# Issue order in a decoder trunk's attention and delta-rule stage: transposes and scores of a head pair next to each other

## The reference, cut to what matters

```python
s = jnp.einsum('bqhd,bkhd->bhqk', qn, k_nope) + jnp.einsum('bqhr,bkr->bhqk', qp, k_pe)
p = jax.nn.softmax(where(k_pos <= q_pos, s * scale, -inf), axis=-1)
o_a = jnp.einsum('bhqk,bkhd->bqhd', p, v)
...
sol = lax.linalg.triangular_solve(system, rhs, left_side=True, lower=True)   # per chunk
v_new = u_c - w_c @ state
o_c = q_c @ state + a_c @ v_new
state = state * exp(gl_c) + kd_c.T @ v_new
```

## Time and profile before

| | us |
|---|---|
| median of 3 runs | 2609.85 |
| lowest, highest | 2607.31, 2614.17 |
| the profiled execution's own time | 2610.53 |
| its span, first to last instruction | 2608.8 |
| PE busy in the span | 2342.1 (90%) |
| DVE, ACT, POOL busy | 1043.6 (40%), 913.8 (35%), 396.4 (15%) |
| mean granted TensorE clock | 0.949 |

### The profile page before, as it was taken

How to read it: one execution, slowest core, us unless ns; L and a number is a source line. 1 busy time by engine, 2 the same in 40 slices (tenths; PEclk the granted TensorE clock), 3 DMA queues, 4 the chain that set the end, 5 groups by cost and what they waited for, 6 DMA issues and landing times. The chain is left out here.

```text
span 2608.8 us, 47837 instructions
## 1 busy us (share of the span) xinstructions
PE 2342.1 (90%) x17450; PEld 1350.2 (52%) x17451; DVE 1043.6 (40%) x2320; ACT 913.8 (35%) x2284; POOL 396.4 (15%) x641
## 2 busy tenths in 40 slices
PE   6999999999588999999998998799974999999990
PEld 2545545555256666666666666355542444444440
DVE  2433433433345656666565556122225222222223
ACT  2273462634545545655554545111110101101103
POOL 1000000000100001000000000122320222222224
PEclk9999999999789999999999989899986999999995
DMA  9122121111443113221212103723321779999777
GB/s 336 71 65 68 47 84 47 59 50 49 128 121 96 59 52 93 82 66 53 69 64 83 36 30 147 266 105 121 116 77 33 211 203 285 283 323 300 230 238 285
DMA packets 187949, 334.34 MB, mean 128 GB/s; under 512 B 19788, under 2 KB 119783, under 8 KB 184567
## 3 DMA queue, kind: packets, MB, share of 16 engines
q1 hardware_dynamic: 173942, 281.51, 31.5%
q0 software_dynamic: 13824, 50.34, 8.0%
HBM read 242.36 MB, written 89.44 MB: 127 GB/s over the span
## 5 line engine op out<-in xcount | busy, mean ns | idle before, releaser
L688 PE MATMUL pV<-mod_rows_then_work,w_in_sb 128*128 128x512 f32 x768 | 340.4, 596 | 5.0 <-ACT mod_rows_then_work L357 5.0
L1416 PE MATMUL scores<-keys_values_then_all,queries 96*128 96x512 f32 (+3 forms) x640 | 311.0, 569 | 23.3 <-DMA keys_values_then_all<-v_d 23.3
L2030 PE MATMUL hidden_ps<-w,keys_values_then_all 128*128 x752 | 331.0, 593 | 0.1
L1136 ACT ACTIVATE probs<-scores,neg_max 128x512 f32<-128x512 f32 (+3 forms) x320 | 199.7, 624 | 341.9 <-DVE neg_max L1264 224.4
L688 PEld LDWEIGHTS pV<-mod_rows_then_work,w_in_sb 128*128 128x128 f32 x768 | 144.6, 191 | 178.0 <-issue 172.0
L2030 PEld LDWEIGHTS hidden_ps<-w,keys_values_then_all 128*128 128x128 f32 x752 | 143.0, 190 | 180.2 <-issue 180.2
L1617 PE MATMUL out_ps<-keys_values_then_all 128*128 128x512 f32 x512 | 227.8, 604 | 2.6 <-ACT keys_values_then_all L1560 2.6
L1421 PE MATMUL bank<-ident,probs 128*128 128x128 f32 x1088 | 188.0, 289 | 1.3 <-ACT probs L1136 1.1
L1264 DVE TENSOR_REDUCE neg_max<-scores 128x1 f32<-128x512 f32 x192 | 132.3, 689 | 133.0 <-PE scores L1416 131.7
L1431 PE MATMUL outT_ps<-probs_T,keys_values_then_all 128*64 128x128 f32 x2176 | 159.7, 286 | 28.5 <-issue 17.3
L1960 ACT ACTIVATE keys_values_then_all<-hidden_ps 128x256 f32<-128x256 f32 x47 | 18.1, 385 | 453.9 <-PE hidden_ps L2030 453.9
(11 more groups left out here) (361 smaller groups left out, 3283.1 us busy)
## 6 DMA issues: line engine op xcount, KB each, us to landing
w<-in_w_dram SPq DMA_DIRECT2D x64, 1024.0 KB
w_sb<-in_w_dram SPq DMA_DIRECT2D x32, 1024.0 KB
w_mod_rows<-in_w_mod_dram SPq DMA_DIRECT2D x16, 1024.0 KB, 4.9
kqv<-qkv_d SPq DMA_DIRECT2D x16, 768.0 KB, 4.4
mod_rows_then_work<-in_w_mod_dram SPq DMA_DIRECT2D x4, 2048.0 KB, 15.0
x_in<-in_x_dram SPq DMA_DIRECT2D x16, 512.0 KB, 4.9
qkv_d<-l_out SPq DMA_DIRECT2D x32, 256.0 KB, 2.3
keys_values_then_all<-y_d SPq DMA_DIRECT2D x16, 512.0 KB, 4.7
```

The source lines that it names most:

```text
L688: last = pe.matmul(pV[n % 2][:], win[:, k, QKV0 + c * P:QKV0 + (c + 1) * P], hT[:, s % 2, k, :], start=(k == 0), stop=(k == ND - 1))
L1136: act.activation(prob[:, e, 0:w].rearrange("p t k -> p (t k)"), pS[e][:, 0:w * P], ACT.Exp, scale=-1.0, bias=nmin[:, i % 2, h, b:b + 1], a ...
L1416: pe.matmul(pS[e][:, 0:w * P], qT[:, i % 2, slot(h)], kT[:, 4 * b:4 * b + w, slot(h), :], start=True, stop=True).then_inc(s_ready, 1)
L2030: last = pe.matmul(pH[par][:], xT[par][:, k], m.w13[:, ds(slot, 1), k].rearrange("p s n -> p (s n)"), start=(k == 0), stop=(k == ND - 1))
```

## The change

In the atoms, the two transposes of an entry become one atom of twice the cost, and the scores of both heads of the next entry another, so an entry's order goes from T0, S0, T1, S1 to T0, T1, S0, S1. In the steps, `VT` gets the cost 0 and `KD` both costs, so no atom comes between them. The sums of the costs stay as they are, and so does every instruction; its place in the queues changes, and with it the banks that the second pass hands out.

```diff
     for j, (i, hp, b) in enumerate(pairs):
         n = min(4, TILE[i] + 1 - 4 * b)
         ahead = min(4, TILE[pairs[j + 1][0]] + 1 - 4 * pairs[j + 1][2]) if j + 1 < len(pairs) else 0
-        for e in range(2):
-            atoms.append((0.11 * n, [("T", j, e)]))
-            if ahead:
-                atoms.append((0.22 * ahead, [("S", j + 1, e), ("X", j + 1, e)]))
+        atoms.append((0.22 * n, [("T", j, 0), ("T", j, 1)]))
+        if ahead:
+            atoms.append((0.44 * ahead, [(kind, j + 1, e) for e in range(2) for kind in "SX"]))
...
-        steps += [(0.45, ("VT", c)), (0.45, ("KD", c)), (1.0, ("KS", c)), (0.7, ("QS", c)), (0.85, ("TR", c))] * rec
+        steps += [(0.0, ("VT", c)), (0.9, ("KD", c)), (1.0, ("KS", c)), (0.7, ("QS", c)), (0.85, ("TR", c))] * rec
```

## The result

| | before | after |
|---|---|---|
| median of 6 runs, us | 2611.13 | 2629.39 |
| lowest, highest | 2607.31, 2614.95 | 2625.10, 2634.22 |
| ratio, with its 95% interval | | 1.0067 [1.0052, 1.0083] |
| the profiled execution's own time | 2610.53 | 2634.22 |
| `mix`, first score to last PE group, us | 922.0 | 945.8 |

The changed kernel is 18 us slower. Its profiled execution was its slowest, 4.8 us above its median, so the traces differ by 23.7 us, and `mix` alone by 23.8: nothing moved in another stage.

What follows compares the result with a forecast made beforehand. PE's queue was taken to bound `mix`, busy 845 of 936 us. The terms 13 + 15 + 2 - 12 - 4.5 - 2 - 3.5 gave +8 on the profiled 2610.5: 2618.5 us, range 2597 to 2640.

Steps and rivals of the forecast that it cites:

- V behind T1: V's wait for DVE's copy of T1's bank: more PE work in between (its cover), 12 us gained, ends 5 and 17.3.
- T behind S: Transposes waiting for the exponentials of their scores: less PE work in between, 13 us lost, ends 8 and 25.
- The need of 1.85 us: PE work needed between a score and its transposes, so that maximum, exponential and sum finish without PE waiting.
- the count of covers: Sum over the step lists of PE work between feeding and waiting groups; T's shortfalls go from 1.1 to 11.6 us.
- Levels: Delta rule's Y and WU: larger atoms leave some steps nothing ahead of them, 15 us lost, ends 9 and 24.
- VT and KD: Turns of values and keys taking two banks at once behind T0 and T1: 2 us lost, ends 0 and 5.
- Seams: PE's changes of tile shape fall from 688 to 637: 4.5 us gained; new same-kind seams free, at most 16 us.
- W0: Its wait for U0 in DVE's full queue: new stalls ahead take from it, 2 us gained, ends 0 and 4.
- The clock: PE's granted clock in mix: one net fall less, 3.5 us gained, ends 14 lost and 14 gained.
- Faster because V's cover decides: Rival: V's largest wait goes and short covers elsewhere turn out enough, -15 us, 2596; chance 0.27.
- Much slower: Rival: exponentials become PE's bound if T needs over 2.1 us of cover, +37 before small terms, 2640; chance 0.12.
- No change that can be told: Rival: the terms cancel within the 7.8 us a measurement can tell, 2610; chance 0.31.

Runs made afterwards that it cites:

- e1: The kernel before with the new order T0, T1, S0, S1, each still an atom of its own, values and keys as before: 2619.98 us, ratio 1.0041.
- e2: The kernel before in its old order T0, S0, T1, S1, with T and S of one head in one atom: 2619.58 us, ratio 1.0050.
- e11: The kernel before with DVE's two steps that wait for ACT cut in two, the waiting half placed later: 2601.75 us, ratio 0.9968.
- e5: The changed kernel with at least one atom placed between level steps that would follow each other at once: 2615.82 us, ratio 1.0028.
- e3: The changed kernel without its second part, VT and KD at 0.45 each as before: 2632.15 us, ratio 1.0090.
- e7: The kernel before with U0, the DVE step that W0 waits for, moved up behind KD: 2590.54 us, ratio 0.9925.
- e4: The kernel before with both transposes in one atom and the scores in two, order T0, T1, S0, S1: 2618.85 us, ratio 1.0048.
- e6: The changed kernel with U0, the DVE step that W0 waits for, moved up behind KD: 2610.89 us, ratio 1.0006.
- e9: The changed kernel run once more without an edit, for a second trace: 2636.62 us.

## Why the prediction was right in its direction and short in its size

The direction and the range held: 2629.39 lies in 2597 to 2640, on the side that had 0.42. The size did not: 8.7 us over the median were forecast, 18 were measured.

- **V behind T1:** -12 forecast for "issue", 17.3 to 5.1 measured, -12.2. e1 shows that the order alone does it (5.6) and e2 that less cover undoes it (32.5). "V's wait is a wait for DVE's copy" holds; that it came from DVE standing still for ACT holds for a third of it (e11).
- **T behind S:** +13 forecast, +9.8 measured (T 1.1 to 10.9). The need of 1.85 us, and not a smaller one, fits: the wait is 10.7 in 19 places, not near 1. But in e1 the same order with single atoms costs 21 where the count of covers gave about 11, so that the count came near in the lump is in part luck. Why the lump halves the wait no run took apart.
- **Levels:** +15 forecast, +8.7 measured (24.9 to 33.6), just under the lower end of 9. Two exponentials in a row ahead of the copy stand in 7.0 us of these waits; e5, which parts the level steps, takes 9.4 us of others out and leaves T alone. Steps with nothing between are not the only source: e2 has one such place where after has 12, and 32.6 us of levels' waits.
- **VT and KD:** +2 forecast, +1.8 of idle in the trace. e3 against after shows no gain from leaving that part out.
- **Seams:** the new ones, S to S and T to T, cost nothing, as taken. Start to start a pair of scores of four tiles is 1.72 us, twice 0.86, and a pair of transposes 0.87, twice 0.44, as in these lines of after:

```profile
914.21 1.16 PE L1396 MATMUL bank<-v_new,qk_transposed 128*128 128x128 f32 x8
915.21 1.88 PE L1415 MATMUL scores<-keys_values_then_all,queries 96*128 96x512 f32 x4
916.93 0.39 PE L1437 MATMUL bank<-ident,out_T 128*128 128x128 f32 x2
```

```profile
1129.75 1.04 PE L1420 MATMUL bank<-ident,probs 128*128 128x128 f32 x8
1130.62 1.45 PE L1415 MATMUL scores<-keys_values_then_all,queries 96*128 96x512 f32 x3
```

  The Trainium skill, TensorEngine Tiling (Array Packing), Key Properties, has the engine drain when the tiling mode changes and not when only the tile does; these pairs, all in one mode, agree with it. The upper end of 16 us is out. The saved changes of shape (688 to 637) were put at -4.5; the work column gives -1.4, and -3.0 in the second traces.
- **W0:** -2 forecast, +2.2 measured: the sign was wrong. `U0` does sit in DVE's full queue, but W0's wait grew all the same; that a stall ahead of it delays `U0` as much as W0 is my reading, and no run took it apart. Its wait is worth most of what can be won in this stage: e7.
- **The clock: this is the step that failed.** "Three followed V's wait for DVE. I take one net fall less: 3.5 us gained; ends 14 lost and 14 gained." The traces show five falls more (10 to 15) and 17 us lost, 22 in the second pair; the runs show 13.7, at the upper end of the 14 lost. The count that it started from was a little off too: one of the ten falls came behind 1.5 us and not 1.6 or more, and the ten lost 29 us together, 2.9 each and not 3.5. The three falls behind V's waits were counted, less two for all that is new; 13 and 15 us of new waits stood in the same sum, and their share of falls, by the rate of before (33.2 us lost to 76.1 idle), would alone have been 12. e1 and e3 settle that it is the clock: idle 84.4 and 82.6, lost clock 32.5 and 49.3, medians 12 us apart, where e1 has even 5.7 us more work. e4 against e3 puts 11 us of it on the pair of scores. Of the +18, the traces and the runs give the clock about two thirds (17.0 of 23.8, 13.7 of 20), and half if only 0.7 of each lost us is paid.

By the sum of its measured terms the forecast would have been 9.8 + 8.7 + 1.8 - 13.6 (all of V) + 2.2, less 0.7 for the others (`K`'s wait fell by 1.7, which is chance), so +8.2 of idle, then 17 of clock and -1.4 of work. My net of idle alone was 13 + 15 + 2 - 12 - 2 = +16: twice too high. That the 8 us too many there hid a part of the clock's error, of 17 to 20 us with its sign, is luck.

**The rivals.** Faster because V's cover decides: V's gain came in full, and was not enough. Much slower: T's need is not over 2.1, as its wait is 10.7 and not 25; the reason of that rival fell, though its block of two exponentials is real, at the levels and not at T. No change that can be told: the idle time alone would nearly have given it.

**What stays open.** Which idle brings a fall. W0 of chunk 14 waited 2.3 us in both kernels: in before the clock fell behind it, in after it did not. V of entry 40 waited 1.65 us in both: in before the clock stayed, in after it fell and cost 5.1 us. The same list of steps, before's, lost 33.2 and 27.3 us. In the traces kernels with the pair of scores lost 36.7 to 50.2 us (after, e3, e5, e6, e9), those without 18.8 to 40.4, so the two sets overlap at e6 and e7; over the runs they don't, if barely (140.0 to 149.9 against 124.3 to 138.8). That the pair raises the loss is shown; by which waits is argued from two places, and e5, which parts stacked waits, takes back about half of it over the runs (147.2 to 140.7). Nor does the count of shape changes explain the work column better than to some 10 us: e1 has 688 as before does, and 817.0 where before has 812.7; e2 has 630 and after 637, with 801.1 and 811.3.

## What to carry to other kernels

When the steps of one chain are put together into a lump, look at what the lump does in the other engines' queues: two exponentials in a row put 1.5 us ahead of a copy of 0.26 that PE waits for. Where TensorE is nearly always busy, a wait can cost more than its length, and a sum that prices new waits must price the clock they may bring too: here 8 us of idle came with 14 to 17 of clock in one kernel, and with none in another (e1). The clock's loss differs from run to run, so take it from the granted clock of many runs before believing one trace. And look first for a small step with no cost of its own that sits late in a full queue (`U0` here): moving that one line was worth 19 us, more than any regrouping.

## What the runs showed of the hardware that was not expected

- The clock fell from 2.4 to 1.2 GHz in a stage where PE is busy nine tenths of the time: in before ten times behind idles of PE of 1.5 to 2.9 us, in after eleven times behind 1.6 to 3.3 us and four times behind nothing longer than 1.35. By slices of 2 us it stayed low for 4 to 14 us and cost 1.7 to 6.8 each time. With these falls, 9 to 15 of them, the stage lost 27 to 50 us in before and after, more than any one wait.
- Two waits close together, 1.07 and 1.35 us with 0.45 us of work between, were followed by a fall, in both traces of after; 1.07 and 0.63 with a score between (e1) were not.
- Start to start at full clock, with a group of another tile shape ahead, a score of four tiles takes 0.96 us where it takes 0.86 behind its own shape, and a transpose of four tiles 0.49 where it takes 0.44; ahead of a small-tile step both take 0.09 longer. e2, which has no score behind another shape, has 12 us less of work.
- The time of one kernel spreads with its clock: before's 26 runs beside e1 to e4 ranged over 23 us (2598.57 to 2621.93), and over all 69 runs the time and the lost clock go together with a correlation of 0.92.
